# Constant products on TensorE at the stage boundaries of a two-block transformer kernel

## What is computed

```python
def second_block(x, ...):
    for l in range(DEPTH_2):
        h = rms_norm(x, norm_mix_w[l])
        x = x + hybrid_mixer(h, ...)
        h = rms_norm(x, norm_ffn_w[l])
        x = x + conv_glu_ffn(h, ...)
    return rms_norm(x, norm_final_w)
```

## Time and profile before

| | |
|---|---|
| median of 3 executions | 2389.31 us (2389.24 to 2395.49) |
| profiled execution, its own time | 2386.79 us |
| its span, first to last instruction | 2385.0 us |
| TensorE busy with matmuls | 2047.3 us (86%), 9656 matmuls |
| VectorE, ScalarE, GpSimd busy | 1395.0, 994.6, 980.6 us |
| mean granted clock of TensorE | 0.936 of full speed |

### The profile page before, as it was taken

The page is one execution under the profiler, slowest core; times in us unless marked ns, Lnnn a source line. Parts: engine busy times, 40 slices in busy tenths (PEclk is TensorE's granted clock), DMA queues, the critical chain, the costliest instruction groups (busy, mean ns, idle before and its releaser), DMA issues.

```text
span 2385.0 us, 26693 instructions
## 1 busy us (share of the span) xinstructions
PE 2047.3 (86%) x9656; PEld 1505.9 (63%) x9656; DVE 1395.0 (58%) x2697; ACT 994.6 (42%) x1756; POOL 980.6 (41%) x562
## 2 busy tenths in 40 slices
PE   6898698778788777777799989989989988998998
PEld 1486467763333333333489777789978976777997
DVE  2785674466666676675336645257753673434776
ACT  1430334321212121211345677355554567744554
POOL 1162246554444444444377547610027844781000
PEclk9899799889989899899999999999989999998999
DMA  8141355459999999999655344445545533453552
GB/s 325 39 141 46 129 210 187 139 235 422 422 421 421 421 421 421 421 421 422 217 166 171 109 144 156 158 146 186 188 139 163 185 106 124 159 184 116 188 188 102
DMA packets 111012, 534.37 MB, mean 224 GB/s; under 512 B 12448, under 2 KB 12576, under 8 KB 77344
## 3 DMA queue, kind: packets, MB, share of 16 engines
q1 hardware_dynamic: 66960, 244.72, 31.1%
q0 software_dynamic: 38720, 275.96, 28.1%
q10 hardware_dynamic: 5200, 11.98, 1.6%
HBM read 531.49 MB, written 1.11 MB: 223 GB/s over the span
## 4 chain that ended last, share of the span: by engine, by line
PE 54%; DMA 24%; DVE 8%; ACT 7%; issue 4%; POOL 3%; ACTq 0%; DVEq 0%; SPq 0%; POOLq 0%
PE psum L791 53%; DMA pair_rows<-in_peer_uv,arena 10%; DMA arena<-in_peer_uv,arena 6%; DMA wring<-in_peer_uv,arena 5%; POOL w_lo L2369 2%; ACT w_hi L1251 2%; ACT arena L1262 1%; DVE arena L1619 1%; PE psum L839 1%; ACT arena L1510 1%; DMA wring<-in_w_ada 1%; ACT arena L1455 1%; DMA dve_junk<-acs_rows 1%; ACT a_hi L1258 1%; DVE dve_junk L1619 1%
## 5 line engine op out<-in xcount | busy, mean ns | idle before, releaser
L2369 POOL TENSOR_TENSOR w_lo<-wring,w_hi 128x1024 fp32r<-128x1024 f32 x282 | 697.9, 2489 | 729.7 <-ACT w_hi L1251 687.9
L1251 ACT ACTIVATE w_hi<-wring 128x1024 fp32r<-128x1024 f32 (+1 forms) x414 | 431.6, 1051 | 357.4 <-PE psum L791 311.7
L791 PE MATMUL psum<-w_hi,a_hi 128*128 128x512 f32 (+1 forms) x1056 | 425.1, 403 | 31.8 <-POOL w_lo L2369 20.7
L791 PE MATMUL psum<-w_lo,a_hi 128*128 128x512 f32 (+1 forms) x1056 | 415.5, 393 | 0.0
L791 PE MATMUL psum<-w_hi,a_lo 128*128 128x512 f32 (+1 forms) x1056 | 415.4, 393 | 0.0
L791 PE MATMUL psum<-arena 128*128 128x512 f32 (+7 forms) x1142 | 342.7, 458 | 81.9 <-ACT arena L1403 45.2
L791 PE MATMUL psum<-a_hi,w_hi 128*128 128x256 f32 x1312 | 377.7, 288 | 11.0 <-POOL w_lo L2369 3.8
L791 PE MATMUL psum<-a_lo,w_hi 128*128 128x256 f32 x1312 | 376.3, 287 | 0.0
L791 PE MATMUL psum<-a_hi,w_lo 128*128 128x256 f32 x1312 | 376.0, 287 | 0.0
L791 PEld LDWEIGHTS psum<-arena 128*128 128x128 f32 (+2 forms) x1142 | 186.5, 200 | 224.9 <-issue 159.0
L791 PE MATMUL psum<-pair_rows,arena 128*128 128x512 f32 x512 | 260.6, 663 | 67.3 <-ACT arena L1403 67.3
(11 more groups left out here) (227 smaller groups left out, 2328.0 us busy)
## 6 DMA issues: line engine op xcount, KB each, us to landing
wring<-in_w_up SPq DMA_DIRECT2D x88, 512.0 KB, 3.3
wring<-in_w_xbc SPq DMA_DIRECT2D x48, 512.0 KB, 3.3
wring<-in_w_dn SPq DMA_DIRECT2D x44, 512.0 KB, 3.3
wring<-in_w_adaT SPq DMA_DIRECT2D x32, 512.0 KB, 4.0
wring<-in_w_qkv SPq DMA_DIRECT2D x32, 512.0 KB, 3.5
wring<-in_w_z SPq DMA_DIRECT2D x32, 512.0 KB, 3.5
wring<-in_w_g SPq DMA_DIRECT2D x32, 512.0 KB, 3.4
wring<-in_w_ps SPq DMA_DIRECT2D x32, 512.0 KB, 3.3
```

The source lines that it names most:

```text
L791: mm = lambda o, a, b, start, stop: nc.tensor.matmul(o, a, b, start=start, stop=stop, skip_group_check=True)
L1251: a.reaches(A(w_hi[:, n % SPLIT_RING, 0:width], wring[:, c % RING, 0:width], ACT.Copy), hi_ready, n + 1)
L2369: nc.gpsimd.tensor_tensor(w_lo[:, r, 0:width], wring[:, c % RING, 0:width], w_hi[:, r, 0:width].bitcast(F32), ALU.subtract).then_inc(lo_re ...
```

## The change

A new helper, `idle_products(name, n)`, takes a bank in the usual order (it is a group of its own in the list) and multiplies the identity with the first 512 columns of the constants, in float32, `n` times; the results stay in the bank and nobody reads them. The last but one product itself raises the `bank_read` of its bank. The helper is called ahead of each of the boundaries' waits, with 28 products at naT, 4 at mT, 9 at hfT, 5 at L0.hT and 7 at L1.hT, 4 at either layer's mT and 6 at either fT.

```diff
@@ psum_order
-    add("naT", 8), add("nacT", 4)
+    add("idle_na"), add("naT", 8), add("nacT", 4)
...
-    add("mix", 8), add("mT", KD), add("gb", 2), add("wout", 4)
-    add("hfT", KD), add("hfrow", 4), 
+    add("mix", 8), add("idle_m"), add("mT", KD), add("gb", 2), add("wout", 4)
+    add("idle_hf"), add("hfT", KD), add("hfrow", 4)
...
-        add(L + "hT", KD), add(L + "qkv", 8), add(L + "small", 2), add(L + "xbc", 24)
+        add(L + "idle_h"), add(L + "hT", KD), add(L + "qkv", 8), add(L + "small", 2), add(L + "xbc", 24)
...
-        add(L + "mT", KD), add(L + "wo", 4)
-        add(L + "fT", KD), add(L + "up", 2 * FT), add(L + "dn", 4)
+        add(L + "idle_m"), add(L + "mT", KD), add(L + "wo", 4)
+        add(L + "idle_f"), add(L + "fT", KD), add(L + "up", 2 * FT), add(L + "dn", 4)
@@ the stream of TensorE
+        def idle_products(name, n):
+
+            o = open_(name, 0)
+            for j in range(n):
+                m = mm(o, ident, consts[:, 0:512], True, True)
+                if j == n - 2:
+                    m.then_inc(read_value(name, 0)[0], 1)
+            close(m)
...
+        idle_products("idle_na", 28)
         pe.wait_ge(S("na_rows"), 1)
...
+        idle_products("idle_m", 4)
         pe.wait_ge(S("merged"), 1)
...
+        idle_products("idle_hf", 9)
         pe.wait_ge(S("scaled"), 2)
...
+            idle_products(L + "idle_h", 7 if l else 5)
             pe.wait_ge(S("scaled"), 3 + 2 * l)
...
+            idle_products(L + "idle_m", 4)
             pe.wait_ge(S("merged"), 2 + l)
...
+            idle_products(L + "idle_f", 6)
             pe.wait_ge(S("scaled"), 4 + 2 * l)
```

## The result

The changed kernel takes 2374.2 us (median of 6, 2371.35 to 2383.06) against 2388.0 for the kernel before (6 runs beside it): ratio 0.9943, 95% interval 0.9921 to 0.9965. So the gain is 10 to 14 us. The first time lies in the stated range by 0.2 us (its lower end was 2374), and the likeliest case said 6 us and "no change", while the gain is beyond the 7.2 us from which the prediction speaks of faster: it lies between the sum and rival (a).

What follows compares the result with a forecast made beforehand. TensorE was taken to bound the kernel, its clock being what the change can touch. Gains of 3.5 and 10.6 us less 6.4 and 1.5 made 6.2 us, 2383.1 off the median of 2389.31; range 2374 to 2392.

Steps and rivals of the forecast that it cites:

- the likeliest case: Whole kernel: 6.2 us less, within the 7.2 us counted as no change; chance 0.56, of which 0.18 beyond 7.2 us.
- the 7.2 us: Whole kernel: about 0.3%, the smallest difference a measurement tells from no change; faster means below 2382.1 us.
- the sum: Whole kernel: 3.5 + 10.6 - 6.4 - 1.5 = 6.2 us less, giving 2383.1 off the median.
- rival (a): Gaps behind the transposes: the clock holds at 1.00 at nearly all boundaries; gain 14.1 us, 2375.2; chance 0.20.
- Rival (c): The nine waits: the clock doesn't take idle products for work and falls under them; 27 us more, 2416; chance 0.06.
- A product costs 0.86 us: The nine waits: 73 float32 products at full clock, 0.86 us each, all within their waits, so they cost nothing.
- The gap behind the transposes: Seven boundaries: TensorE stands about 1.2 us longer there; four clock falls of 1.6 us each give back 6.4 us.
- 1 us lost there: At naT: scores wait for a transfer's bias, so faster transposes bring nothing, and a clock fall costs 1 us.
- The transposes' term: Seven boundaries, mT and the L ones: transposes at full clock gain 0.5 us each, 3.5 us in all.
- 10.6 us lost now: Products behind seven boundaries: 22.6 us busy at half clock, times 0.47, which a clock that never fell would give back.
- two to six falls: Behind the seven boundaries: the number of clock falls for the forecast's own range, 2379 to 2387 us; four taken.
- The chance of 0.38 for faster: Whole kernel: chance of a time below 2382.1 us, against 0.56 for same and 0.06 for slower.

Runs made afterwards that it cites:

- f4: The nine groups with two products of only 8 columns each, waits left empty, against the kernel before: 2384.23 us, ratio 1.0001.
- f1: The changed kernel measured again, unchanged, against the kernel before: 2374.24 us, ratio 0.9959.
- g3: The changed kernel measured once more, unchanged, against the kernel before: 2376.25 us, ratio 0.9948.
- e3: The changed kernel plus 2 or 3 idle products in the gap behind the transposes of seven boundaries: 2366.65 us, ratio 0.992 to the kernel before.
- e1: The changed kernel with eight float32 128x128 transposes in place of each idle product: 2377.44 us, ratio 0.9965 to the kernel before.
- f3: The changed kernel with two idle products more in each of the nine waits: 2384.01 us, ratio 0.9997 to the kernel before.
- f2: The changed kernel with only naT's 28 products, none at the eight other boundaries: 2381.5 us, ratio 0.9989 to the kernel before.
- e4: The changed kernel without naT's 28 products and their group: 2380.14 us, ratio 0.9971 to the kernel before.

## Why the prediction was right and wrong

The traces give the time from the last product group ahead of a boundary to the first groups of products behind it (at mT, L0.mT and L1.mT to the last ones of their short stage), between the same two records in every trace. Means over two traces with empty waits (before, f4) and three of the changed kernel (after, f1, g3), in us:

| boundary | empty | changed | difference | e3 |
|---|---|---|---|---|
| naT | 33.61 | 31.85 | -1.76 | 31.84 |
| mT | 35.17 | 33.52 | -1.64 | 32.33 |
| hfT | 18.75 | 19.03 | +0.28 | 19.39 |
| L0.hT | 23.58 | 23.38 | -0.20 | 21.36 |
| L0.mT | 31.77 | 31.00 | -0.77 | 30.47 |
| L0.fT | 23.98 | 23.65 | -0.33 | 22.16 |
| L1.hT | 25.05 | 23.17 | -1.88 | 22.74 |
| L1.mT | 32.35 | 31.52 | -0.84 | 30.44 |
| L1.fT | 24.10 | 23.71 | -0.39 | 22.16 |
| all nine | | | -7.5 | |
| the rest of the kernel | | | -2.7 | |

**Right.** The bound and the lever: TensorE's clock, not its waits. f4 and e1 show that it is the work in the wait, whatever it computes, that brings the gain. A product costs 0.86 us, and all counts fit their waits. Rival (c) didn't come: the clock takes these products for work. An overrun is paid, as f3 shows. The gap behind the transposes grows by 0.8 to 1.2 us, and the clock falls there again, four times in the profiled execution as the sum had it (six and five times in f1 and g3), and e3 shows that this was what was left to gain.

**Wrong, step by step.**

- That at naT "the scores wait for a bias that VectorE adds at 259.81 once a transfer has landed", so that faster transposes bring nothing, and 1 us lost there. This is the step that failed in kind. I took the last event of a wait for several as its cause. It was the second head's bias; the first scores waited for ScalarE's copies, and these follow the transposes. Instead of losing 1 us naT gave 1.8, 2.8 us that the sum lacks. The fall that I put at 1 us came in none of the eight traces with naT's wait filled.
- The transposes' term, 0.5 us a boundary. At hT and fT the first product starts some 0.5 us sooner (5.2 to 5.6 became 4.7 to 5.2), as taken. At the mT boundaries, where the low parts are not scaled, 5.0 to 5.1 became 4.1 to 4.2: 0.9 us, since VectorE writes such a low part in 0.33 us and not in the 0.4 that I carried over from another instruction. Some 1.2 us too little over three boundaries, and less where half of the transposes ran at full clock already, as at L0.mT before.
- "10.6 us lost now" was read from one execution, and it was a bad one. It had 25.3 us of half clock behind the seven boundaries in products, f4 has 18.2, with none at L0.mT and L1.mT. The changed kernel's three traces have 13.7, 23.1 and 17.1. So this term is (21.8 - 18.0) x 0.47 = 1.8 us net, against the 10.6 - 6.4 = 4.2 of the sum. Right in kind, twice too large by these traces. Even that is not clear of chance: f2, whose seven waits are empty too, has 17.2, and e4, where they are filled, 17.1. In the same way "two to six falls" was right, and their number differs from execution to execution.
- The rest of the kernel had no term. Its 2.7 us are a sum of parts that go both ways. The query products and key scores behind hfT, up to the first product of gathered rows, take 1.9 us less (91.6 became 89.7), where before and f4 show 13.7 us at half clock and the changed kernel's traces 10.2. But f2, with hfT untouched, has 10.2 too and 89.3, and e3, with hfT filled, has 91.1. So it isn't the fill at hfT; what made the difference there stays open, and so does chance. The stage between L0.hT and L0.mT takes 2.3 us less in the mean, but 345.2 to 350.0 us in single traces, and e1 and e4, with the waits filled, have 349.9 and 349.4. The expert stage behind takes 0.9 us more, and the part ahead of naT 0.5.

The sum over profiled executions is then 10.2 us (7.5 at the boundaries, 2.7 without a shown cause), which the medians of three measurements (13.8, 9.6, 11.5) bracket. So the mechanism was right, and the 6.2 us are a sum in which naT, the transposes and the rest were too small by some 6.5 us in all and the products behind too large by 2.4. That the first time fell into the range, with 0.2 us to spare, owes something to luck. The chance of 0.38 for faster was too low: the sum stood 1 us short of that line, and naT alone would have carried it over.

## What to carry to other kernels

Where TensorE comes to a stage boundary at full clock, the cost of a wait is not only the wait: the transposes, the copies that follow them and the first products behind it run at half clock. Constant work of a known price fills it, but it must reach up to the end of the wait without passing it (half the fill brought a third to a half of the gain, two products too many took all of it). The next gap behind the transposes must be filled too: with both the gain was some 19 us where the waits alone brought 10 to 14. Before a term is set to nothing because "it waits for X", look for what else the same wait needs, and when that is through.

## What the runs showed of the hardware that was not expected

- Float32 transposes alone held the full clock: 223 in 24.5 us at 1.00 (e1), and by the ratios the time was within 5 us of that with products.
- The intervals between the same two points mostly repeat to 0.3 us in executions in which the clock falls at the same places, and differ by steps of about 0.8 to 2 us where it doesn't: L1.mT took 30.44 to 30.49 us in five traces of filled waits without a fall behind the transposes and 32.03 to 32.07 in two with one. That the spread of this kernel's executions (2378.9 to 2395.5) is in good part where its falls land is my reading; no run shows it.
- Constant products that end inside a wait cost nothing there: the time from the last real product to the first transpose was the same to 0.02 us in before and f4 and in the three traces of the changed kernel at eight of the nine boundaries (26.03 and 26.04 us at naT). At mT it was 4.82 and 4.83 against 4.84 to 5.15.
- At L0.fT and L1.fT the changed kernel fell behind the transposes in all three traces (TensorE stands 3.10 us there), at the mT boundaries (2.1 to 2.2 us) in five of nine cases.
